# Two transformer blocks on one core: norm roots applied at the eviction for the attention norms, an unscaled first pair for the conv FFN, and weight splits ahead of the eviction

## The reference

```python
def rmsnorm(x, g):
    return x * lax.rsqrt(jnp.mean(x * x, axis=-1, keepdims=True) + EPS) * g

def conv_ffn(h, w_up, conv_w, conv_b, w_down):
    u = h @ w_up                              # 1024 -> 2 * 2816
    u = conv3_along_tokens(u, conv_w) + conv_b
    g, up = jnp.split(u, 2, axis=-1)
    return (jax.nn.silu(g) * up) @ w_down

x = first_block(...)          # mods: silu(c) @ ada_w[i] + ada_b[i]; returns _rms_norm(hx, final_g)
for l in range(2):            # second block
    h = rmsnorm(x, attn_norm[l])
    c_q, c_kv, k_r, q_d, k_d, v_d = split(h @ w_in[l])
    o_a = mla_mixer(c_q, c_kv, k_r, ...)      # norms of c_q and c_kv first, then attention
    o_b = dilated_attention(rmsnorm(q_d), rmsnorm(k_d), v_d, ...)
    x = x + concat(o_a, o_b) @ w_out[l]
    x = x + conv_ffn(rmsnorm(x, ffn_norm[l]), w_up[l], conv_w[l], conv_b[l], w_down[l])
```

## Time and profile before

| | |
|---|---|
| median of 3 runs | 1957.94 us (1956.85 to 1967.49) |
| the profiled execution's own time | 1951.73 us |
| its span | 1950.0 us |
| mean granted PE clock | 0.954 of full |
| busy: PE, DVE, ACT, POOL | 1787.7, 1099.0, 835.6, 282.9 us (92%, 56%, 43%, 15%) |
| chain that ended last | PE 82%, DVE 9%, ACT 3%, DMA 2%, POOL 2% |

### The profile page before, as it was taken

The page is one execution under the profiler, slowest core; times in us unless marked ns, Lnnn a source line. Parts: engine busy times, 40 slices in busy tenths (PEclk is TensorE's granted clock), DMA queues, the critical chain, the costliest instruction groups (busy, mean ns, idle before and its releaser), DMA issues.

```text
span 1950.0 us, 32080 instructions
## 1 busy us (share of the span) xinstructions
PE 1787.7 (92%) x12422; PEld 1592.3 (82%) x12422; DVE 1099.0 (56%) x2077; ACT 835.6 (43%) x1579; POOL 282.9 (15%) x195
## 2 busy tenths in 40 slices
PE   4799999899999989997899988888999887889998
PEld 2697778588888869975799977778999877789998
DVE  0516654644443453357556553685877636858775
ACT  1426653423232342336444443464645434646453
POOL 2200002100000032100100010602322106023221
PEclk9899989999999999999899997899999989999999
DMA  9325572333333333346266641512666515126663
GB/s 296 110 66 174 182 209 98 97 97 97 97 98 97 97 108 98 106 132 196 70 188 176 187 123 52 173 45 82 178 175 190 143 49 175 45 79 180 175 188 94
DMA packets 405877, 254.55 MB, mean 131 GB/s; under 512 B 8064, under 2 KB 404640, under 8 KB 405728
## 3 DMA queue, kind: packets, MB, share of 16 engines
q1 hardware_dynamic: 404576, 248.80, 43.5%
q0 software_dynamic: 1152, 3.71, 0.7%
HBM read 251.36 MB, written 1.11 MB: 129 GB/s over the span
## 4 chain that ended last, share of the span: by engine, by line
PE 82%; DVE 9%; ACT 3%; DMA 2%; issue 2%; POOL 2%; SPq 0%; DVEq 0%; ACTq 0%; POOLq 0%
PE bank L1708 64%; PE bank L1809 4%; PE bank L1792 3%; PE bank L1801 3%; PE bank L1731 2%; DVE WORK L1471 2%; DMA raw<-ada_w 1%; PE bank L1760 1%; DVE TOK L1617 1%; ACT parts L1071 1%; PE bank L1737 1%; DVE parts L897 1%; PE bank L1687 1%; DVE TOK L1612 1%; PE bank L1787 1%
## 5 line engine op out<-in xcount | busy, mean ns | idle before, releaser
L1708 PE MATMUL bank<-AT,parts 128*128 128x256 f32 (+1 forms) x4656 | 691.7, 311 | 31.6 <-DVE AT L883 16.2
L1708 PEld LDWEIGHTS bank<-AT,parts 128*128 128x128 f32 x4656 | 640.3, 195 | 82.3 <-issue 33.6
L1071 ACT ACTIVATE parts<-raw 128x1024 fp32r<-128x1024 f32 (+1 forms) x368 | 368.0, 1040 | 330.0 <-PE bank L1708 318.9
L897 DVE TENSOR_TENSOR parts<-raw,parts 128x1024 fp32r<-128x1024 f32 (+2 forms) x300 | 415.1, 1409 | 150.6 <-ACT parts L1071 150.5
L1708 PE MATMUL bank<-HID,parts 128*128 128x256 f32 (+1 forms) x2592 | 401.4, 318 | 9.1 <-DVE HID L1419 9.1
L1708 PEld LDWEIGHTS bank<-HID,parts 128*128 128x128 f32 x2592 | 368.9, 193 | 39.8 <-DVE HID L1419 9.7
L1708 PE MATMUL bank<-parts,AT 128*128 128x256 f32 (+1 forms) x2208 | 283.2, 291 | 39.6 <-POOL parts L897 19.9
L1708 PEld LDWEIGHTS bank<-parts,AT 128*128 128x128 f32 x2208 | 277.2, 199 | 46.7 <-issue 33.9
L897 POOL TENSOR_TENSOR parts<-raw,parts 128x1024 fp32r<-128x1024 f32 x68 | 168.2, 2482 | 491.2 <-ACT parts L1071 491.1
L1023 POOL TENSOR_TENSOR WORK<-WORK 128x256 f32<-128x256 f32 (+1 forms) x33 | 43.4, 1316 | 683.4 <-ACT WORK L1103 681.2
L1588 DVE SCALAR_TENSOR_TENSOR H<-bank,MOD,H 128x256 f32<-128x256 f32 x120 | 52.6, 479 | 154.7 <-PE bank L1708 154.7
(11 more groups left out here) (145 smaller groups left out, 1377.5 us busy)
## 6 DMA issues: line engine op xcount, KB each, us to landing
raw<-mlp_w SPq DMA_DIRECT2D x128, 512.0 KB, 4.2
raw<-ada_w SPq DMA_DIRECT2D x96, 512.0 KB, 4.6
raw<-w_up SPq DMA_DIRECT2D x88, 512.0 KB, 4.7
raw<-w_in SPq DMA_DIRECT2D x32, 512.0 KB, 4.7
raw<-w_down SPq DMA_DIRECT2D x32, 512.0 KB, 4.4
raw<-odd_w_in SPq DMA_DIRECT2D x24, 512.0 KB, 3.8
raw<-w_out SPq DMA_DIRECT2D x16, 512.0 KB, 4.0
raw<-even_w_in SPq DMA_DIRECT2D x12, 512.0 KB, 4.5
```

Of the source, the lines that this page charges most:

```text
L897: ng.tensor_tensor(chunk_part(c, 1), chunk_raw(c), chunk_part(c, 0).bitcast(F32), ALU.subtract)\
L1071: return nc.scalar.activation(o, i, ACT.Copy)
L1708: ins = MM(out, stay, move, start=kt == 0 and i == 0, stop=kt == kts - 1 and i == 2)
```

## The change

Five things are changed.

1. **Attention norms.** For the attention norms of both layers of the second block, the `latent` products run on `H` times the gain, without the root. New units `prep` (two tiles each) make these tiles' high and low part and their squares, behind the residual products that finish the tiles. The ones-matmuls (`sums_of`) stand between the two halves of `latent` 0, and a unit `rstd` computes the root. DVE evicts the `latent` results with a multiplication by it; for the `dil` products, where tokens lie on partitions, a unit `turn_r` transposes the root (two PE transposes, one small ACT copy to `RT`), and ACT evicts with two operations of 128x256 in place of one of 128x512. In layer 0 the final norm is folded in: the sums are 512 wide (squares of `H`, and of `H` times `final_g`), `rstd` does Ln, Exp and Newton twice, one after the other, and `H` itself is scaled later (unit `final`, 8 DVE operations behind `latent` 2).
2. **FFN norm.** The first pair of the conv FFN runs on such unscaled tiles too (in the second half of `AT`), with the ones-matmuls between the halves of its gate product. Behind the pair come `rstd`, then `apply` (scaled tiles for all following pairs, as before), then two `taps` units, which evict the two banks: DVE multiplies by the root into `WORK`, then ACT and DVE do the taps from there.
3. **Splits first.** In all `conv` units ACT's and DVE's weight splits stand ahead of the eviction and the taps.
4. **Ada rows** are turned by two PE transposes (each 128x128) and one DVE reduction.
5. The split of a chunk is moved past `apply`, `prep` and `rstd` as well.

```diff
-    mlp(1, False)
-    norm("fin", 0, N, "final_g", dst="H")
+    st = factored("attn", 0, "attn_norm", 2 * N)
+    mlp(1, False, after=st)
 
     for l in range(2):
-        norm("attn", l, N, "attn_norm")
+        prepare(st, 3)
+        statistic(st)
+        add("rstd", ("rstd", "attn", l), layer=l, st=st)
         for n in range(3):
             pan = panel("w_in_2", l, 0, KT, n * PW, PW if n < 2 else 160)
             add("latent", ("latent", l, n), layer=l, n=n, panel=pan)
+            if n == 1:
+                add("turn_r", ("turn_r", l), layer=l, st=st)
+        if l == 0:
+            add("final", ("final",), st=st)
...
-        project_out("w_out_2", l, None, False)
-        norm("ffn", l, N, "ffn_norm")
+        st = factored("ffn", l, "ffn_norm")
+        project_out("w_out_2", l, None, False, after=st)
+        prepare(st, 3)
+        statistic(st)
...
+                    if g + i == 0 and up:
+                        add("rstd", ("rstd", "ffn", l), layer=l, st=st)
+                        add("apply", ("apply", "ffn", l), layer=l, width=N, gain="ffn_norm", src="H", dst="AT", kts=KT,
+                            st=st)
+                        for v in (0, 1):
+                            add("taps", ("taps", l, v), layer=l, st=index[("conv", l, 0, 0, v)])
```

```diff
         put_at = at
-        while put_at + 2 < c.users[0] and units[put_at + 1].kind == "stat":
+        while put_at + 2 < c.users[0] and units[put_at + 1].kind in ("stat", "apply", "prep", "rstd"):
             put_at += 1
```

ACT's share of `prep`, `rstd` and the `conv` and `taps` units:

```diff
+                elif k == "prep":
+                    st = x.st
+                    lo, hi = raw_cols(st)
+                    for kt in prep_tiles(x):
+                        consumed(act, h_tile_unit(pos, kt).u)
+                        nc.scalar.activation(AT[:, 0, kt, lo:hi], H[:, kt, 0:N], ACT.Identity, scale=raw_gain(st, kt))\
+                            .then_inc(raw_high, 1)
+                    for kt in prep_tiles(x):
+                        if st.width == 2 * N:
+                            step(nc.scalar.activation(SQ[:, kt, N:2 * N], H[:, kt, 0:N], ACT.Square,
+                                                      scale=par("final_g", kt)))
+                            settle()
+                        nc.scalar.activation(SQ[:, kt, 0:N], H[:, kt, 0:N], ACT.Square).then_inc(squares_ready, 1)
...
+                        act.wait_ge(final_var, 1)
+                        step(nc.scalar.activation(RSTD[:, st.n % 2, N:2 * N], LNV[:, N:2 * N], ACT.Ln,
+                                                  bias=eps[:, 0:1]))
+                        settle()
+                        nc.scalar.activation(RSTD[:, st.n % 2, N:2 * N], RSTD[:, st.n % 2, N:2 * N], ACT.Exp,
+                                             scale=-0.5).then_inc(final_rstd, 1)
...
-                    copy(DQKV[:, :, x.n * PW:(x.n + 1) * PW], b.rearrange("p (t c) -> p t c", t=TB))\
-                        .then_inc(bank_drained[x.u % BANKS], 1)
+                    consumed(act, index[("turn_r", x.layer)].u)
+                    for tb in range(TB):
+                        ins = nc.scalar.activation(DQKV[:, tb, x.n * PW:(x.n + 1) * PW], b[:, tb * PW:(tb + 1) * PW],
+                                                   ACT.Identity, scale=RT[:, x.layer, tb:tb + 1])
+                        if tb == 0:
+                            step(ins)
+                        else:
+                            ins.then_inc(bank_drained[x.u % BANKS], 1)
...
+                elif k == "conv" or k == "taps":
+                    if k == "conv" and not last_hidden(pos):
+                        high_parts(x)
+                    y = x if k == "conv" else x.st
+                    if k == "taps" or not y.raw_in:
...
-                            ins.then_inc(mid_ready, 1)
-                    if not last_hidden(pos):
-                        high_parts(x)
-                    if not x.up:
-
-                        consumed(act, x.u)
-                        nc.scalar.activation(PT[:, x.c % 2, :], PR[:, x.conv % 4, :], ACT.Tanh, scale=0.5)\
...
+                            filled(act, y.u)
+                            mid = b.rearrange("p (a t) -> p a t", a=2)
+                        exp_set = False
```

DVE's share (in `conv` and `taps`, the low split first, then the multiplication of the raw pair, then the taps):

```diff
-                    V.tensor_tensor(MOD[:, x.layer, 2 * x.n:2 * x.n + 2, :], b[:, 0:4].rearrange("p (a b) -> p a b", b=2),
+                    parts = b[:, 0:2 * P].rearrange("p (t g i) -> p t i g", t=2, g=GROUPS)[:, :, 0:2, :]
+                    if x.c:
+                        consumed(dve, ada_turns[x.c - 1].u)
+                    step(V.tensor_reduce(ADS[:, :, :], parts, AX_X, ALU.add))
+                    settle()
+                    V.tensor_tensor(MOD[:, x.layer, 2 * x.n:2 * x.n + 2, :], ADS[:, :, :],
...
+                elif k == "latent":
+                    filled(dve, x.u)
+                    r = rstd_of(x.norm)
+                    if x.n < 2:
+                        V.tensor_tensor(CQ[:, 2 * x.n:2 * x.n + 2, :], b.rearrange("p (a t) -> p a t", a=2),
+                                        over_tokens(r, 2), ALU.mult).then_inc(drained, 1)
...
+                elif k == "final":
+                    for kt in range(KT):
+                        step(V.scalar_tensor_tensor(H[:, kt, 0:N], H[:, kt, 0:N], par("final_g", kt),
+                                                    RSTD[:, x.st.n % 2, 0:N], ALU.mult, ALU.mult))
...
+                elif k == "apply":
+                    for kt in range(KT):
+                        V.scalar_tensor_tensor(WORK[:, kt, 0:N], H[:, kt, 0:N], gain_ap(x, kt), rstd_of(x.st), ALU.mult,
+                                               ALU.mult).then_inc(scaled, 1)
+                        if kt % 2:
...
+                    y = x if k == "conv" else x.st
+                    if k == "taps" or not y.raw_in:
+                        o = conv_out(y)
+                        mid = bank[:, y.u % BANKS, :].rearrange("p (a t) -> p a t", a=2)
+                        done = bank_drained[y.u % BANKS]
+                        if y.raw_in:
+                            filled(dve, y.u)
+                            V.tensor_tensor(conv_mid(y), mid, over_tokens(rstd_of(y.norm), 2), ALU.mult).then_inc(done, 1)
+                            mid, done = conv_mid(y), taps_done
+
```

PE's share:

```diff
                     consumed(pe, ada_rows[x.c].u)
                     for t in range(2):
-                        last = MM(b[:, 2 * t:2 * t + 2], ADR[:, x.c % 2, t * P:(t + 1) * P],
-                                  CON[:, CONST["group_sum"]:CONST["group_sum"] + 2], start=True, stop=True)
+                        last = nc.tensor.transpose(b[:, t * P:(t + 1) * P], ADR[:, x.c % 2, t * P:(t + 1) * P], ident)
...
+                elif k == "turn_r":
+                    consumed(pe, x.st.u)
+                    r = rstd_of(x.st)
+                    for tb in range(TB):
+                        last = nc.tensor.transpose(b[:, tb * P:(tb + 1) * P], r[:, tb * P:(tb + 1) * P], ident)
                 elif k == "latent":
                     for i in range(2 if x.n < 2 else 1):
+                        if x.n == 0 and i == 1:
+
+                            consumed(pe, x.norm.u - BANKS)
+                            sums_of(x.norm).then_inc(bank_filled, 1)
                         last = split_product(b[:, i * N:(i + 1) * N], x, KT, i * P, P,
                                              lambda kt, part: AT[:, part, kt, 0:N], True, normed)
...
                     for c, i in enumerate((x.t,) if x.wide else (0, 1)):
+                        if c and k == "conv" and x.raw_in and not x.up:
+
+                            consumed(pe, x.norm.u - BANKS)
+                            sums_of(x.norm).then_inc(bank_filled, 1)
```

294 lines of the change are left out of this document (215 added, 79 removed).

## The result

The changed kernel is slower: 1965.66 us median (1957.77 to 1968.68, 20 runs) against 1956.78 (1950.97 to 1968.01, 20 runs), ratio 1.0033, 95% interval 1.002 to 1.0047. By the ratio that is 6.5 us more (8.9 between the medians) where 2.5 us less was forecast. The profiled executions, 1961.5 and 1950.0 us of span, are 11.5 apart, since the one of before took 5.1 us less than its median and the one of the changed kernel 2.2.

A forecast was written before the change was run, and what follows sets the result against it. PE was taken as the bound (busy 92% of the span, 82% of the chain). −8 − 6 + 18 + 2 − 8.5 = −2.5 against the profiled 1951.7 gave 1949.2, with 6.2 for the median 1955 us; range 1935 to 1969.

The forecast's parts named there:

- part 1: Attention norm, layer 0: `latent` products end at 32.3 us for 40.8, despite a new 5.6 us PE wait; −8 us.
- parts 3 and 4: FFN entry and conv loop with splits first: entry gain lost to a weight wait, longer turns; 8.9 us a layer.
- +18: Total forecast cost in us of the FFN entry and the splits-first loop, both layers.
- +0.24 a pair: Conv loop: extra us per pair, from a turn of 12.1 us against 11.9 before.
- the turn of 12.1: Conv loop: us from tanh, splits, taps and `up` operations in one turn, where PE needs 11.75.
- Split start to the end of the low part, 4.70: FFN entry: us for the third unit's splits, putting the fifth product's start at 36.15, 0.55 later.
- −8.5: Ada rows: us saved by transposes for matmuls, −4.5 in the first attention and −4 elsewhere.
- B: Rival: ada rows give nothing, their PE passes having covered softmax work; 1964 us, chance 0.12.
- part 2: Attention norm, layer 1: entry from 31.6 to 25.7 us; about −6, or −3.5 if the short wait drops the clock.
- The `dil` evictions: Attention: two ACT operations for one cost 0.4 us more, six a layer; taken as 1.0 a layer, +2 us.
- A: Rival: the conv loop keeps up, FFN entry and loop give −6 in place of +18; 1931 us, chance 0.22.
- C: Rival: new PE waits in the six conv streaks lower the clock, 13 us more; 1968.6 us, chance 0.16.

The follow-up runs named there:

- noraw: Changed kernel with the FFN norm as before (no unscaled pair), splits still ahead of the eviction: 1953.4 us, ratio 1.0004 to the kernel before.
- attn_ada: Changed kernel with FFN norm and split order as before; only attention norms, dil evictions and ada rows changed: 1931.98 us, ratio 0.9898 to the kernel before.
- noraw_nopool: early_nopool with splits ahead of the eviction in all conv units: 1911.73 us, ratio 0.9783 to the kernel before.
- early_nopool: attn_ada with latent 1's splits ahead of the root and all w_up low parts on DVE: 1909.7 us, ratio 0.9783 to the kernel before.
- late: Changed kernel with weight splits behind eviction and taps again, unscaled pair kept: 1946.28 us, ratio 0.9974 to the kernel before.
- late_nopool: Changed kernel with splits behind the eviction again and no w_up low parts on POOL, unscaled pair kept: 1929.15 us, ratio 0.988 to the kernel before.
- attn_ada_nopool: attn_ada with all w_up low parts on DVE, none on POOL: 1919.11 us, ratio 0.9824 to the kernel before.
- dvelate: Changed kernel with only DVE's low split behind the taps again, ACT's splits still first: 1956.12 us, ratio 1.0017 to the kernel before.
- defer_en: late_nopool with latent 1's splits ahead of the root and the pair's taps behind the third product's splits: 1924.46 us, ratio 0.9851 to the kernel before.
- single: early_nopool with the first gate product alone on unscaled tiles at the FFN entry: 1912.12 us, ratio 0.9795 to the kernel before.
- b_ada: Kernel before with only the ada rows changed: 1946.43 us, ratio 0.9971 to the kernel before.
- early: attn_ada with latent 1's weight splits ahead of the root: 1918.68 us, ratio 0.9822 to the kernel before.
- b_nopool: Kernel before with all w_up low parts done by DVE, none by POOL: 1941.68 us, ratio 0.9941 to the kernel before.
- nopool: Changed kernel with all w_up low parts done by DVE, none by POOL: 1930.77 us, ratio 0.9883 to the kernel before.

## Why the prediction was wrong

**Right:** part 1 nearly to the row (predicted a wait of 5.6 and an end at 32.3; 5.99 and 32.2), and the whole mechanism of parts 3 and 4: PE waits for weights instead of tiles, before the fifth product, and the gain of the entry is gone. Newton's end, split start and clock price came as put (split start 31.4 predicted, 30.8 measured from 1333.1; 1.8 of 2.2).

**Mis-sized, and what decided the sign: "+18" for parts 3 and 4.** The two FFNs cost 26.2 us, 13.1 a layer for 8.9; with that alone in its place the sum is +5.7 and not −2.5. By streak of layer 0, from PE's rows, it is 7.6 for 4.6, 3.8 for 2.0 and 1.5 for 2.3. Two terms were too small.

- *"+0.24 a pair", the turn of 12.1.* The turns cost 2.1 us in streak 1 and 2.2 in streak 2, for 0.7 each: two turns of streak 2 are 13.4 and 12.4 us long, for 12.1. My sum for a turn had one operation held up, the low part. The trace has POOL's hold on whatever operation with two SBUF inputs DVE runs beside POOL: `up` operations (2.78 for 0.69) and the pair's taps, which now read `WORK` in place of PSUM (2.97 for 0.88), as well as the low part; the loop's own taps, which read PSUM, keep their 0.87. The start of the down products behind streaks 1 and 2 costs 1.6 us for 1.2, two new waits of 0.6 among it.
- *"Split start to the end of the low part, 4.70", at the entry.* I took it from the row of a loop turn, where DVE is free when the high part is done. After the `taps` units it isn't: two taps and two `up` operations were still ahead, and it took 6.5 (1363.95 to 1370.43). The fifth product began at 37.6, not 36.15; with the clock's 1.8 us for 2.2 taken off, this is 1.0 us a layer.

The Trainium skill's rule ("SBUF — State Buffer", "Who interferes with whom") pointed at this: it speaks of any VectorE operation with two SBUF inputs, and the `up` operations and the pair's taps have them, the loop's taps not. The trace agrees in all three. I applied it to the subtraction alone.

**Shown as causes**, by kernels that remove one each: the order of the splits (21 us in two layers by noraw against attn_ada, FFN 10.4 a layer), and that POOL's share makes it dear (2.3 a layer by noraw_nopool against early_nopool); the pair (15 us by late against attn_ada), most of which stays without POOL's share (11 us by late_nopool against attn_ada_nopool).

**Not shown apart:** that POOL's share costs by the hold alone. Taking it away also replaces POOL's own subtraction of 2.4 us by one of 1.2 on DVE. PE's new waits are for DVE's low parts and the held rows stand ahead of them, which speaks for the hold; dvelate, where 4.7 us a layer stay with no held operation in the loop, shows that ACT's order has a price of another kind when DVE's taps stand ahead of its low part. No run has dvelate without POOL's share.

That the pair's price is the backlog of the `taps` units is shown as far as the place goes: the wait follows the taps (defer_en), and halves with half of them (single). What single leaves open is why an unscaled product doesn't pay even then; the lower clock of that stretch is seen, and its share wasn't tried apart.

**Too high: "−8.5" for the ada rows.** They gave 5.7 (b_ada). Two transposes take 0.38 us where 0.33 was put, and in the first attention (144 to 301 us) all of them 10.0 where the matmuls took 14.4: PE's work there falls by the 4.5 that were put, but the stretch only by 2.5. The part that B named is in this: PE's waits for the score chain's ACT operations go from 0.7 to 1.5 us. What took the rest the rows don't show. The Trainium skill ("TensorE: Matmul & The Clock Gate", "Part 4: PE-mode transpose") has about 275 ns for one transpose in a kernel, by which this part would be nothing; with 0.19 here the measurement decides against it. The granted clock of the stretch is 1.00 with the transposes as it was with the matmuls.

**Small:** part 2 gave 4.4 for 6, because the short wait dropped the clock (48 matmuls in 7.47), the case that the prediction gave 3.5 for. The `dil` evictions (+2 forecast) show −0.8 and +1.1 in the two attentions, within what these profiles differ by: where the edits leave the first block alike, its end comes anywhere from 1148.7 (early) to 1150.6 us (defer_en).

**Rivals:** A (the loop keeps up) is wrong: it does so only without POOL's share, and even there the changed FFN takes 211.4 us against b_nopool's 206.0. That nopool's 1930.8 is A's time is luck, since much of it is what POOL's share cost before as well. B is wrong by b_ada. C's clock is wrong as a cause: the stretches of the loop stand at 1.00. The measured 1965.7 lies inside the stated 1935 to 1969, on the side that was put there for C; that it does is luck too, since C's mechanism isn't what cost the time.

**The parts as measured**, −8.6 − 4.4 + 26.2 + 0.3 − 5.7 (b_ada), add to +7.8, between the 6.5 of the ratio and the 8.9 of the medians.

## What to carry to other kernels

Before putting a step first in an in-order queue, ask what holds it and what then stands behind it: here the held low part was cheap as the last step of a unit and dear as the first. Work given to GpSimd isn't free because GpSimd is idle: here it lengthened VectorE operations with two SBUF inputs beside it, and taking it back was worth 0.6% on the kernel before and 1.5% on the changed one, by one line. A norm moved behind its product leaves its evictions to be done while the next weights are due: count what stands ahead of the next split, not only the wait that goes.
